# Query and mixing features: the high weights against both parts of the input in one 512-column product

## What is computed

```
ul = (xl * (1 + sc1_l) + sh1_l) @ w_in          # one input projection for all branches
ya = head_rms_norm(hgrn(q, k, logf, v)) * silu(g)   # q: "query"; g: "mix" panels 0 to 3
yc = attention(rope(cq), ...)                       # cq: "mix" panels 4 to 7
yb = pool_mixer(b)                                  # b:  "mix" panels 8 to 11
xl = LN(alpha*xl + g1 * (sum_j sigmoid(gate_j) * (y_j @ w_branch_j)) @ w_out)
xl = LN(alpha*xl + g2 * relu(h @ w1)**2 @ w2)
```

## Time and profile before

| | |
|---|---|
| median of 3 runs | 1875.08 us (1874.62 to 1876.07) |
| profiled execution, its own time | 1874.27 us |
| its span | 1872.5 us |
| PE, DVE, ACT, POOL busy | 99%, 69%, 44%, 15% |

### The profile page before, as it was taken

How to read it: one execution, slowest core, us unless ns; L and a number is a source line. 1 busy time by engine, 2 the same in 40 slices (tenths; PEclk the granted TensorE clock), 3 DMA queues, 4 the chain that set the end, 5 groups by cost and what they waited for, 6 DMA issues and landing times.

```text
span 1872.5 us, 24733 instructions
## 1 busy us (share of the span) xinstructions
PE 1846.6 (99%) x10052; PEld 1564.1 (84%) x10052; DVE 1285.3 (69%) x1501; ACT 833.0 (44%) x1026; POOL 273.0 (15%) x159
## 2 busy tenths in 40 slices
PE   6999999999999999999999999999999999999998
PEld 3679888899999877888888888888888888888886
DVE  3357777776868775577767667776686468547887
ACT  3242244465464554454444445443344344434442
POOL 0000000005655262001001000220012001100100
PEclk9999999999999999999999999999999999999999
DMA  9987755443434454565776754565665556656652
GB/s 397 418 352 271 270 203 196 170 172 136 158 108 163 167 175 147 188 257 202 271 268 225 282 209 160 225 247 198 252 239 210 196 209 227 223 192 234 229 184 105
DMA packets 60465, 408.94 MB, mean 218 GB/s; under 512 B 6464, under 2 KB 9280, under 8 KB 12352
## 3 DMA queue, kind: packets, MB, share of 16 engines
q1 hardware_dynamic: 55872, 395.60, 58.2%
q10 hardware_dynamic: 4480, 11.76, 1.7%
HBM read 405.24 MB, written 2.10 MB: 218 GB/s over the span
## 4 chain that ended last, share of the span: by engine, by line
PE 90%; DVE 4%; DMA 3%; DVEq 2%; ACT 0%; SPq 0%; issue 0%; ACTq 0%
PE main L1547 14%; PE main L1545 14%; PE main L1546 14%; PE side L1520 6%; PE main L1520 6%; PE main L1460 5%; PE main L1462 5%; PE main L1461 5%; PE main L1524 3%; PE side L1524 3%; DMA raw<-in_w_ad 3%; DVE wlo L989 1%; DVEq L1128 1%; DVE lv L1122 1%; PE side L1579 1%; PE main L1601 1%
## 5 line engine op out<-in xcount | busy, mean ns | idle before, releaser
L989 DVE TENSOR_TENSOR wlo<-raw,whi 128x1024 fp32r<-128x1024 f32 x542 | 697.5, 1313 | 297.5 <-ACT whi L496 296.6
L496 ACT CAST whi<-raw 128x1024 fp32r<-128x1024 f32 x541 | 562.4, 1050 | 701.1 <-PE main L1547 389.3
L1460 PE MATMUL main<-hCL,whi 128*128 128x256 f32 (+1 forms) x768 | 248.1, 323 | 1.0 <-DVE wlo L989 1.0
L1462 PE MATMUL main<-hCL,wlo 128*128 128x256 f32 (+1 forms) x768 | 244.9, 319 | 0.0
L1461 PE MATMUL main<-hCL,whi 128*128 128x256 f32 (+1 forms) x768 | 244.8, 319 | 0.0
L1010 DVE SCALAR_TENSOR_TENSOR asum<-raw,sm,asum 128x512 f32<-128x512 f32 x240 | 211.5, 881 | 19.9 <-issue 0.9
L1547 PE MATMUL main<-whi,hid 128*128 128x512 f32 x496 | 193.3, 390 | 0.0
L1546 PE MATMUL main<-wlo,hid 128*128 128x512 f32 x496 | 193.3, 390 | 0.0
L1545 PE MATMUL main<-whi,hid 128*128 128x512 f32 x496 | 193.2, 390 | 0.0
L1520 PE MATMUL side<-h,whi 128*128 128x512 f32 x512 | 160.9, 396 | 0.0
L1545 PE MATMUL main<-whi,hCL 128*128 128x512 f32 x384 | 156.3, 407 | 0.6 <-DVE wlo L989 0.6
(11 more groups left out here) (283 smaller groups left out, 2905.7 us busy)
## 6 DMA issues: line engine op xcount, KB each, us to landing
raw<-in_w_f SPq DMA_DIRECT2D x128, 1024.0 KB, 4.9
raw<-in_w_in SPq DMA_DIRECT2D x103, 1024.0 KB, 4.9
raw<-in_w_ada SPq DMA_DIRECT2D x64, 1024.0 KB, 4.9
raw<-in_w_ad SPq DMA_DIRECT2D x32, 1024.0 KB, 15.5
raw<-in_w_br SPq DMA_DIRECT2D x24, 1024.0 KB, 5.1
raw<-in_w_out SPq DMA_DIRECT2D x16, 1024.0 KB, 4.9
xin<-in_xT SPq DMA_DIRECT2D x8, 512.0 KB, 18.5
raw<-in_w_ck SPq DMA_DIRECT2D x4, 512.0 KB, 14.5
```

The source lines that it names most:

```text
L496: nc.scalar.copy(half_at(q)[0], slots[slot][:, 2 * h:2 * h + 2]).then_inc(hi_made, 1)
L989: TT(half_at(q)[1], slots[slot][:, 2 * h:2 * h + 2], half_at(q)[0].bitcast(F32), ALU.subtract).then_inc(lo_made, 1)
L1460: mm(out, w_hi, x_hi, start=start, stop=False)
L1462: return mm(out, w_lo, x_hi, start=False, stop=stop)
```

## The change

In query and mix, the two products with w_hi become one of 512 columns: the moving operand is `x[:, kt, :, lo:hi]`, both parts of the tile as two runs of 256, and the result fills a whole bank, w_hi·x_hi in its first half and w_hi·x_lo in its second. The product w_lo·x_hi is added to the first half. So the two halves of a bank still have to be added: ScalarE copies the second half to SBUF (`halves`), VectorE adds the first half to it (`sums`), and with that the bank is free. All eight calls are now emptied in this way. The gate of the recurrence goes through a new tile `zg`: tanh is taken from it, and the multiplication by it is one instruction over four banks, at k = 4.

```diff
@@ panels()
-    pn.add("query", 0, 4, four, "A")
+    pn.add("query", 0, 4, four, "V")
     pn.add("query", 4, 4, four, "V")
     for i in range(2):
-        for n, who in enumerate("VAV"):
-            pn.add("mix", 12 * i + 4 * n, 4, four, who)
+        for n in range(3):
+            pn.add("mix", 12 * i + 4 * n, 4, four, "V")
@@ ScalarE
+            def halves(name, first, out):
+                for b in range(4):
+                    blk(name, first, b)
+                    nc.scalar.copy(out[:, b], main[:, b, T:2 * T]).then_inc(half_in, 1)
+
...
                 if k == 3:
-                    for b in range(4):
-                        blk("query", 0, b)
-                        nc.scalar.copy(q_t[:, b], main[:, b, 0:T]).then_inc(freed["A"], 1)
+                    halves("query", 0, q_t[:, 0:4])
...
+            halves("query", 4, q_t[:, 4:8])
...
                 drain()
+                act.wait_ge(freed["V"], PN.own["mix", 12 * h + 4] + 4)
                 nc.scalar.copy(qs[0:64], g4[64:128])
...
                     if k == 3:
+                        halves("mix", 12 * i, zg)
                         for b in range(4):
-                            blk("mix", 12 * i, b)
-                            A(ya[:, i * 4 + b], main[:, b, 0:T], ACT.Tanh, scale=0.5).then_inc(gs_sig, 1)
+                            act.wait_ge(freed["V"], PN.own["mix", 12 * i] + b + 1)
+                            A(ya[:, i * 4 + b], zg[:, b], ACT.Tanh, scale=0.5).then_inc(gs_sig, 1)
                     if k == 7:
-                        for b in range(4):
-                            blk("mix", 12 * i + 4, b)
-                            nc.scalar.copy(cq[:, i * 4 + b], main[:, b, 0:T]).then_inc(freed["A"], 1)
+                        halves("mix", 12 * i + 4, cq[:, 4 * i:4 * i + 4])
...
+                        if i:
+                            act.wait_ge(y_done, 1)
+                        halves("mix", 12 * i + 8, xb[:, 4 * i:4 * i + 4])
@@ VectorE
+            def sums(name, first, out):
+                before = first if name == "query" else 8 + first
+                for b in range(4):
+                    dve.wait_ge(half_in, before + b + 1)
+                    TT(out[:, b], out[:, b], main[:, b, 0:T], ALU.add).then_inc(freed["V"], 1)
+
             for k in range(8):
                 split_after("query", k)
                 if k < 4:
                     gate_block(3, k, True)
-            for b in range(4):
-                blk("query", 4, b)
-                nc.vector.tensor_copy(q_t[:, 4 + b], main[:, b, 0:T]).then_inc(freed["V"], 1)
+                if k == 3:
+                    sums("query", 0, q_t[:, 0:4])
+            sums("query", 4, q_t[:, 4:8])
...
                     if k == 3:
-                        for b in range(4):
-                            blk("mix", 12 * i, b)
-                            dve.wait_ge(gs_sig, i * 4 + b + 1)
-                            STT(ya[:, i * 4 + b], ya[:, i * 4 + b], 1.0, main[:, b, 0:T], ALU.add,
-                                ALU.mult).then_inc(freed["V"], 1)
+                        sums("mix", 12 * i, zg)
+                    if k == 4:
+                        dve.wait_ge(gs_sig, i * 4 + 4)
+                        out = ya[:, 4 * i:4 * i + 4]
+                        STT(out, out, 1.0, zg[:], ALU.add, ALU.mult)
+                    if k == 7:
+                        sums("mix", 12 * i + 4, cq[:, 4 * i:4 * i + 4])
                     if k == 11:
-                        for b in range(4):
-                            blk("mix", 12 * i + 8, b)
-                            nc.vector.tensor_copy(xb[:, i * 4 + b], main[:, b, 0:T]).then_inc(freed["V"], 1)
+                        sums("mix", 12 * i + 8, xb[:, 4 * i:4 * i + 4])
@@ TensorE, features()
+                            own = slice(P * b, P * (b + 1))
+                            if both:
+                                for j in range(2):
+                                    kt = 4 * n + 2 * h + j
+                                    mm(parts(main, b), whi[:, par, j, own], x[:, kt, :, lo:hi],
+                                       start=kt == 0, stop=kt == 15, skip_group_check=True)
+                                for j in range(2):
+                                    kt = 4 * n + 2 * h + j
+                                    last = mm(main[:, b, 0:T], wlo[:, par, j, own], x[:, kt, 0, lo:hi],
+                                              start=False, stop=kt == 15, skip_group_check=True)
```

More of the change, by code:

```diff
@@ L367, in build @@
         o_r = [xb[:, 4:8], lv[1][:, 1]]
+        zg = at("zg", [P, 4, T], 212 * KB)
         avg = at("avg", [P, 4, HD], 208 * KB)
@@ L408, in build @@
          at_v, at_sc, at_max, at_exp, at_norm, at_tr, at_cp, at_o, at_y, y_hi, y_lo, pool_diff, pool_ps, pool_y, m_done,
-         m_tr, m_hi, m_lo, ax_in, var_in, rs_out, nm_out, h2_tr, h2_hi, h2_lo, x1_done, hid_in, hid_pos, hid_hi, hid_lo, y_out, cleared, sum_hi, sum_lo, centred, diag_made, scaled, row_out, vals_in) = (
+         m_tr, m_hi, m_lo, ax_in, var_in, rs_out, nm_out, h2_tr, h2_hi, h2_lo, x1_done, hid_in, hid_pos, hid_hi, hid_lo, y_out, cleared, sum_hi, sum_lo, centred, diag_made, scaled, row_out, vals_in, half_in) = (
             sem(x) for x in (
@@ L414, in build @@
             "at_v at_sc at_max at_exp at_norm at_tr at_cp at_o at_y y_hi y_lo pool_diff pool_ps pool_y m_done "
-            "m_tr m_hi m_lo ax_in var_in rs_out nm_out h2_tr h2_hi h2_lo x1_done hid_in hid_pos hid_hi hid_lo y_out cleared sum_hi sum_lo centred diag_made scaled row_out vals_in").split())
+            "m_tr m_hi m_lo ax_in var_in rs_out nm_out h2_tr h2_hi h2_lo x1_done hid_in hid_pos hid_hi hid_lo y_out cleared sum_hi sum_lo centred diag_made scaled row_out vals_in half_in").split())
         n_done = [sem("n_done_first"), sem("n_done_second")]
@@ L1462, in three, with parts @@
                 return mm(out, w_lo, x_hi, start=False, stop=stop)
+            def parts(ps, b):
+                return ps[:, b].rearrange("p (v t) -> p v t", v=2)
             def features(name, first, x, lo, hi, ready=None, between=lambda k: None, middle=lambda k: None):
+                both = hi - lo == T
                 for n in range(4):
@@ L1473, in features @@
                                 bank(name, first, b)
[L1474 to L1478, removed]
+                            own = slice(P * b, P * (b + 1))
[8 more added lines that the diff above has]
+                                              start=False, stop=kt == 15, skip_group_check=True)
+                            else:
+                                for j in range(2):
+                                    kt = 4 * n + 2 * h + j
+                                    last = three(main[:, b, 0:hi - lo], whi[:, par, j, own], wlo[:, par, j, own],
+                                                 x[:, kt, 0, lo:hi], x[:, kt, 1, lo:hi], kt == 0, kt == 15)
                             if n == 3 and h == 1:
@@ L1485, in features @@
                     between(n)
-            def parts(ps, b):
-                return ps[:, b].rearrange("p (v t) -> p v t", v=2)
             def ahead(name, first, ps, n, h, blocks):
```

## The result

The changed kernel takes 1891.69 us (median of 4 runs, 1890.96 to 1893.31), the one before 1875.57 us in the runs beside it: a ratio of 1.0087, with a 95% interval of 1.0075 to 1.0099. It is slower, as forecast, but by 16.1 us instead of 7, outside the range. The profiled execution has a span of 1890.1 us against 1872.5.

A forecast was written before the change was run, and what follows sets the result against it. PE was taken as the bound by under 2 us, with DVE right behind. -5.9 + 2.8 + 1.4 + 8.4 - 1.2 + 1.5 = +7.0 us gave a median of 1882 us, range 1876.5 to 1887.5.

The forecast's parts named there:

- PE's rate: Query and mix: each of 512 triples takes 0.0115 us less with the 512-column product, -5.9 us.
- query 0 to query 4: Query 4's first bank waits for DVE's additions, which stand behind the gate block of k = 3: +2.8 us.
- operand 4, both i: Mix 0 to mix 4: later tanh and the gate multiplication delay operand 4, 0.7 us for each i, +1.4 us.
- banks ahead of mix 8 and 20: Mix 4's bank additions stand on DVE behind panel 8's low parts and level 5's scores: 4.2 us each i, +8.4.
- the old waits at mix 9 and 21: PE's existing wait for the low part at mix 9 goes, since DVE and POOL have caught up: -1.2 us, both i.
- operand 3, i = 1: In mix, operand 3 waits on ScalarE's exponential, which four tanh delay some 1.5 us; no separate price.
- gates: ACT's copies delay its swap, so POOL's rotation falls on DVE's low parts: +1.5 us, bounds 0 and 3.
- The sum: The step adding all terms to +7.0 us: 1881.3 us for the profiled execution, 1882 for the median.
- What would show it: Trace signs: 0.3485 us pairs, gaps of 2 to 3 us at query 4, 3 to 5 us before mix 8 and 20.
- the second: DVE without POOL: L989 returns to 2.35 us for two, mix 4 banks cost 0.8 each; -2.2 us, 1873; 12%.
- the third: Faster: DVE keeps its lead over operand 6, wait at mix 8 below 0.3 us; -3.7 us or better, 1871; 7%.
- the fourth: The wide product gains nothing, two runs of 256 costing what two products cost: 1888; 9%.

The follow-up runs named there:

- e9: Changed kernel, with PE forming the scores of level 6 three times instead of once in both halves of mix: 1890.08 us (1.0076).
- e8: Changed kernel, ScalarE alone emptying mix 4 and 16 (addition at k = 10), query 0's additions first, swap first, gate multiplication at k = 9: 1875.12 us.
- e5: Changed kernel, with the 1024-column multiplication by the gate at mix k = 9 instead of k = 4: 1891.43 us (1.0088).
- e1: Changed kernel, with VectorE adding the halves of mix 4's banks before the low parts of panel 8: 1885.81 us (1.0053).
- e2: Changed kernel, with ScalarE doing swap(0) before the four copies of mix 20's second halves: 1885.62 us (1.0053).
- e7: Changed kernel, with ScalarE alone emptying the banks of mix 4 and 16 and VectorE adding in one instruction at k = 10: 1884.97 us (1.0056).
- e3: Changed kernel, with VectorE adding query 0's halves before the gate block of k = 3: 1888.05 us (1.0064).
- e4: Kernel before, with the changed product order alone, banks emptied as before, w_hi times x_lo left out in query and mix: 1872.13 us (0.9982).
- e10: Changed kernel, ScalarE alone emptying mix 4 and 16, query 0's additions first, swap first, gate multiplication and cq addition at k = 11: 1872.36 us (0.9985).

## Why the prediction was right in sign and wrong in size

The cause, bank additions that stand on VectorE behind other work, was forecast and shown. By the terms of the sum, in the profiled executions:

| term | forecast | measured |
|---|---|---|
| PE's rate | -5.9 | -5.8 |
| query 0 to query 4 | +2.8 | +3.3 |
| operand 4, both i | +1.4 | +2.5 |
| banks ahead of mix 8 and 20 | +8.4 | +8.0 |
| the old waits at mix 9 and 21 | -1.2 | -1.5 |
| operand 3, i = 1 | 0 | +0.3 |
| gates | +1.5 | +4.2 |
| the clock | not in the sum | +5.9 |
| sum | +7.0 | +16.9 (spans: +17.6) |

The measured entries are differences between PE's starts in the two traces. The clock's is what the products behind the three gaps took longer than the same products at 2.4 GHz: 1.45 and 1.55 us in mix and 2.9 us at the gates (from 642.48, the first product of gates 2, to 650.93, where 628.18 to 633.75 stood before). That is less than half of the 13.7 us at 1.2 GHz, in part because PE was still idle for 0.9 us of them. Most of the 0.7 us that the sum lacks arises behind the gates; I did not follow it further.

**The step that failed** is "The sum": it took each wait at its length. "What would show it" named gaps of 3 to 5 us ahead of mix 8, and nowhere did the prediction ask what the granted clock does behind such a gap. It said "PE is busy 99% of the span at the full granted clock" and left it there. A wait of 4.0 us cost 5.5. e9 shows this by itself for the gaps in mix: with the same moment of release and PE busy, the slow stretch is gone. With this term at 5.9 the forecast would have been 1888, still under the 1891.69 that were measured: it is the largest part of the miss but not all.

**Mis-sized terms.** The gates: the term of +1.5 with its bounds 0 and 3 saw that the rotation would fall on DVE's low parts, but not that it would also fall on the four multiplications of ya, 4.61 us instead of 1.67; the measured 4.2 is outside the bounds. The operand of level 4: the multiplication by the gate takes 2.07 us in both halves, not 1.2 (at k = 9 in e8 it takes 1.21, with POOL's level work done); the upper bound had this value and I didn't take it. Operand 3 was named as one that ScalarE's tanh would delay, but got no price of its own; in i = 1 it costs 0.3 us. Query 4: 0.5 us more, 0.4 of it because the gate block itself began later, at 400.35 instead of 399.94 us.

**What was right.** The rate, to 0.1 us, with the two runs of 256. The banks ahead of mix 8, 4.0 us against 4.2, and that other calls' banks cost nothing: no gap at mix 4, mix 12 or the first call of mix. The old wait at mix 9 is gone. Of the rivals, the second and the third are out (the wait is there), and so is the fourth (the rate is there).

The argument for the 4.2 was in part wrong, though: I had the lead of operand 6 used up by earlier delays. In the trace it ends 1.08 us ahead of its products, and e5 shows that taking the delays away leaves the wait the same. The number came out because the low parts kept their 4.97 us: 6.8 - 1.7 - 1.08 is 4.0, by the prediction's own sum with the lead that the trace shows. So the wait's cause was right and its size in part luck. Two sums in the prediction are off without changing a term: 6.39 + 0.42 + 0.06 is 6.9 and not 6.8, and the swap moves by 5.1 us from 610.34 to 615.4, where the text says about 4.5.

## What to carry to other kernels

When one engine's operation is replaced by a pair on two engines, the price is not the operation but the place at which the second engine comes to it in its order: here four additions of 0.41 us cost 3 to 4 us each time, and moving them by one place gave back 3.3 us at query 4 and 2.8 of 4.0 us at mix 8. If a forecast contains a wait of several microseconds of TensorE, add what the clock may take behind it (1.5 us behind most of the gaps here, up to 2.9 us at the gates), and look at the clock in windows of 2 us, since a row of 47 us slices hides it. And where VectorE and GpSimd share a stage, read durations at the place where an operation will stand, not where it is undisturbed.

## What was not expected of the hardware

The clock's fall is not the same for the same wait. Behind query 4's gap of 3.4 us it stayed up in the changed kernel's profile and fell in those of e1, e2, e5, e7 and e9. Behind the gaps of 4.0 us in mix it fell both times in the changed kernel and in e3, and once of two in e2. Behind the gap of 4.3 us at the gates it fell in all six profiles that have one, for 3.4 or for 6.8 us. Behind the gap of 2.5 us near 730 us it fell in those of e4, e8 and e10, and not in those of the kernel before and e7. So a shorter gap can bring it down where a longer one doesn't. I did not settle what decides it; the runs of one kernel differ by up to 3 us, perhaps in part for this reason; that isn't shown.
